# Pooling in a two-block transformer kernel: shifted sums on the vector engines replaced by a constant matrix behind the group weights

## The chip, the cores and the metric
The kernel runs on one core of a Trainium2 chip. The metric is the device time of one execution in microseconds (us); 2959.66 is the median of three runs of the kernel before.

## What is computed
Two blocks of layers work on 256 latent tokens and 256 context tokens of width 1024. The change touches the mixer of the first layer alone, which runs once, on all 512 tokens:

```python
def pool_mix(h, w, scale):                       # h: normalised, modulated
    ...
    for gi, win in enumerate(POOL_WINDOWS):      # 2, 4, 8, 16
        lo = jnp.clip(t - win // 2, 0, n - 1)
        hi = jnp.clip(t - win // 2 + win - 1, 0, n - 1)
        sl = slice(gi * POOL_GW, (gi + 1) * POOL_GW)
        csg = cs[:, :, sl]
        mean = (csg[:, hi + 1] - csg[:, lo]) / (hi - lo + 1)
        outs.append(mean - hf[:, :, sl])
    diff = jnp.stack(outs, axis=2)
    y = jnp.einsum('bngc,gce->bnge', diff, w).reshape(b, n, d)
    return y * scale
```

Each of four groups of 256 features takes the mean over a window of neighbouring tokens, less the token itself, and is then multiplied by its own 256x256 weights. The result, gated, is added to x. A feed-forward layer (ffn 0) runs ahead of it and another (ffn 1) behind it, each after an RMS norm.

## The kernel before, in words
Activations lie feature-major: a tile has 128 features on the partitions and 512 tokens (256 latent, 256 context) along the row; `x` has eight of them. Every large product is made of three f32r matmuls (`mm3`, lines 1995 to 1997): an operand is split into a high part (`hh`, `whi`, written by ScalarE) and the rest (`hl`, `wlo`, written by VectorE), and low x high, high x low and high x high add up in PSUM. Sums of squares (L2010), idle matmuls that only keep TensorE's clock up (`keep_clock`, L2002) and attention use plain fp32 matmuls, each of which shows as two records in the trace.

Each engine has its program written by hand in order, and semaphores join them. Weights come through three slots of 1 MB (`wraw`); SyncE loads a slot when VectorE has split the chunk that was in it (L614, waiting on `w_lo`), ScalarE copies it into `whi` (L718) and VectorE subtracts (L1147).

A norm: as each tile of `x` is final, ScalarE squares it (L722), TensorE adds the squares over the features (`sum_squares`, L2010); ScalarE takes the root (L739), VectorE the reciprocal (L1173). VectorE then scales 16 half tiles (L1181), ScalarE adds the shift (L757). In the mode "split", ScalarE's result goes into `hh`, and VectorE, three half tiles behind its own scaling, writes `hl` (L1193) and signals `h_ready`; TensorE can start with the first half tiles. In the mode "plain", used ahead of the pooling only, the result goes back into `tsq`, no `hl` is written, and VectorE waits for all 16.

The pooling before: `pool_group` (L505 to L518) copies a group of 128x1024 into a padded buffer, adds it to a shifted copy of itself once, twice, three or four times (windows 2, 4, 8, 16), multiplies by a table of reciprocals and subtracts the input. VectorE does groups 0, 1 and 3, GpSimd group 2. ScalarE rounds each result into `hh` (L1032), VectorE writes the rest into `hl` (L1571, signal `y_ready`), and TensorE makes two tiles of 128x512 for each group from 12 matmuls. VectorE adds each tile to `x` (L1216). TensorE runs 14, 4, 0 and 0 idle matmuls ahead of the four groups, besides the 7 of the norm.

GpSimd's queue also loads the weights of the modulation (`ADA`, 512 KB each) for later feed-forward layers. Since pooling uses the same memory (`scr`), it sends the eight loads for ffn 1 only when the last group has been rounded.

## Time and profile before

| | us |
|---|---|
| median of three runs (2958.22 to 2962.6) | 2959.66 |
| the profiled execution, its own time | 2946.88 |
| its span, first to last instruction | 2945.1 |
| TensorE busy | 2796.8 (95%) |
| VectorE busy | 2062.8 (70%) |
| ScalarE busy | 1022.2 (35%) |
| GpSimd busy | 98.2 (3%) |

The times of rows count from the start of the span. A busy share of the whole span is a mean over many stages; the pooling takes about 2% of it and has to be read by itself. PE is TensorE's matmuls, PEld its weight loads, which run beside matmuls; DVE is VectorE, ACT is ScalarE, POOL is GpSimd. PEclk is the granted clock as a share of 2.4 GHz.

### The profile page before, as it was taken

The page shows a single profiled execution, that of the slowest core. Times are in us where ns is not written, and L with a number is a line of the kernel's source. Part 1 is how long each engine was busy: PE and PEld are TensorE (multiplying, and loading weights), DVE is VectorE, ACT ScalarE, POOL GpSimd, SP SyncE. Part 2 cuts the span into 40 slices and gives each one's busy share as a digit, 9 for nine tenths or more (in the row PEclk, how much of TensorE's full clock was granted, in tenths as well). Part 3 has the DMA queues.
Part 4 walks back from the last instruction along what each step waited for, and adds up shares of the span by engine and source line. Part 5 has one row for each costly group of instructions (what it writes and reads, how often), then busy time and mean ns, then how long its engine had stood idle before and what let it go on. Part 6 is the DMA issues. An engine that isn't in the chain of part 4 may idle for free.

```text
span 2945.1 us, 48427 instructions
## 1 busy us (share of the span) xinstructions
PE 2796.8 (95%) x19022; PEld 2436.4 (83%) x19022; DVE 2062.8 (70%) x3047; ACT 1022.2 (35%) x1148; POOL 98.2 (3%) x160
## 2 busy tenths in 40 slices
PE   6999997999999999999999899998899989998998
PEld 4888864788878888778799899887699979986898
DVE  6877778876677777776667766656656666666566
ACT  5222232222233222233344444452144434443443
POOL 1000002000000000000000000000000000000000
PEclk9999998999999999999999999999999989998999
DMA  8444422444334344322244345421044554443354
GB/s 322 157 158 173 167 79 92 144 151 158 139 114 157 143 154 174 121 100 72 83 182 174 129 172 200 162 85 45 2 156 178 191 131 171 177 165 65 115 189 167
DMA packets 68652, 420.84 MB, mean 143 GB/s; under 512 B 7624, under 2 KB 8776, under 8 KB 26672
## 3 DMA queue, kind: packets, MB, share of 16 engines
q1 hardware_dynamic: 47984, 341.26, 31.5%
q0 software_dynamic: 20576, 78.26, 8.3%
q8 instruction: 69, 1.13, 0.2%
q14 instruction: 23, 0.19, 0.0%
HBM read 418.42 MB, written 1.07 MB: 142 GB/s over the span
## 4 chain that ended last, share of the span: by engine, by line
PE 86%; DVE 8%; ACT 3%; issue 2%; DMA 1%; SPq 0%; ACTq 0%; DVEq 0%
PE ps_o L1995 11%; PE ps_o L1997 11%; PE ps_o L1996 11%; PE ps_u L1995 8%; PE ps_u L1997 7%; PE ps_g L1995 7%; PE ps_u L1996 7%; PE ps_g L1997 7%; PE ps_g L1996 7%; PE ps_g L2010 2%; DVE wlo L1147 1%; PE ps_o L2194 1%; ACT whi L718 1%; DVE rstd L1173 1%; DVE tsq L1181 1%
## 5 line engine op out<-in xcount | busy, mean ns | idle before, releaser
L718 ACT ACTIVATE whi<-wraw 128x2048 fp32r<-128x2048 f32 x323 | 616.3, 1912 | 881.1 <-PE ps_u L1997 406.8
L1147 DVE TENSOR_TENSOR wlo<-wraw,whi 128x2048 fp32r<-128x2048 f32 x323 | 731.5, 2288 | 174.8 <-ACT whi L718 174.5
L1995 PE MATMUL ps_o<-ah,wlo 128*128 128x256 f32 (+1 forms) x1408 | 462.0, 328 | 17.1 <-issue 15.4
L1995 PE MATMUL ps_g<-hh,wlo 128*128 128x256 f32 (+1 forms) x1416 | 456.4, 322 | 20.0 <-DVE hl L1191 13.8
L1995 PE MATMUL ps_u<-hh,wlo 128*128 128x256 f32 (+1 forms) x1416 | 454.6, 321 | 2.2 <-DVE wlo L1147 2.2
L1997 PE MATMUL ps_g<-hh,whi 128*128 128x256 f32 (+1 forms) x1416 | 455.0, 321 | 0.0
L1996 PE MATMUL ps_g<-hl,whi 128*128 128x256 f32 (+1 forms) x1416 | 454.5, 321 | 0.0
L1997 PE MATMUL ps_u<-hh,whi 128*128 128x256 f32 (+1 forms) x1416 | 454.4, 321 | 0.0
L1996 PE MATMUL ps_u<-hl,whi 128*128 128x256 f32 (+1 forms) x1416 | 453.9, 321 | 0.0
L1997 PE MATMUL ps_o<-ah,whi 128*128 128x256 f32 (+1 forms) x1408 | 452.7, 322 | 0.0
L1996 PE MATMUL ps_o<-al,whi 128*128 128x256 f32 (+1 forms) x1408 | 452.1, 321 | 0.0
L1216 DVE SCALAR_TENSOR_TENSOR x<-ps_o,gcol,x 128x256 f32<-128x256 f32 x640 | 283.4, 480 | 146.0 <-PE ps_o L1997 144.3
L1995 PEld LDWEIGHTS ps_g<-hh,wlo 128*128 128x128 f32 x1416 | 267.4, 189 | 48.0 <-issue 27.6
L1995 PEld LDWEIGHTS ps_o<-ah,wlo 128*128 128x128 f32 x1408 | 265.8, 189 | 43.0 <-issue 20.4
L1995 PEld LDWEIGHTS ps_u<-hh,wlo 128*128 128x128 f32 x1416 | 267.2, 189 | 23.3 <-DVE wlo L1147 2.7
L1996 PEld LDWEIGHTS ps_o<-al,whi 128*128 128x128 f32 x1408 | 265.9, 189 | 23.8 <-issue 2.9
L1997 PEld LDWEIGHTS ps_g<-hh,whi 128*128 128x128 f32 x1416 | 267.5, 189 | 20.7
L1996 PEld LDWEIGHTS ps_g<-hl,whi 128*128 128x128 f32 x1416 | 267.5, 189 | 20.3
L1997 PEld LDWEIGHTS ps_u<-hh,whi 128*128 128x128 f32 x1416 | 266.9, 189 | 20.7
L1996 PEld LDWEIGHTS ps_u<-hl,whi 128*128 128x128 f32 x1416 | 267.1, 189 | 20.5
L1997 PEld LDWEIGHTS ps_o<-ah,whi 128*128 128x128 f32 x1408 | 265.6, 189 | 21.0
L806 ACT ACTIVATE ah<-tsq 128x512 fp32r<-128x512 f32 (+1 forms) x88 | 69.8, 793 | 469.8 <-PE ps_o L1997 459.7
(433 smaller groups left out, 3713.3 us busy)
## 6 DMA issues: line engine op xcount, KB each, us to landing
wraw<-in_W SPq DMA_DIRECT2D x324, 1024.0 KB, 4.8
scr<-in_ADA POOLq DMA_DIRECT2D x126, 512.0 KB, 3.9
scr<-bias_rows POOLq DMA_DIRECT2D x8, 384.0 KB, 8.7
x<-in_XT POOLq DMA_DIRECT2D x1, 2048.0 KB, 10.8
x<-in_MEMT POOLq DMA_DIRECT2D x2, 1024.0 KB, 6.2
cst<-in_CST POOLq DMA_DIRECT2D x1, 1511.5 KB, 7.3
cst<-in_CB POOLq DMA_DIRECT2D x1, 1024.0 KB, 5.1
out<-x SPq DMA_DIRECT2D x1, 1024.0 KB, 4.8
```

The source lines that it names most:

```text
L718: nc.scalar.activation(whi[:, n % SLOTS, :], wraw[:, n % SLOTS, :], ACT.Copy).then_inc(w_hi, 1)
L806: nc.scalar.activation(ah[:, :, 0:N], tmp[:, :, 0:N], ACT.Copy).then_inc(a_hi, 1)
L1147: tt_(wlo[:, n % SLOTS, :], wraw[:, n % SLOTS, :], whi[:, n % SLOTS, :].bitcast(f32), sub).then_inc(w_lo, 1)
L1173: nc.vector.reciprocal(rstd[:, 0:N], rstd[:, 0:N]).then_inc(nm_rstd, 1)
L1181: stt(dst, src(d)[:, HALVES[j]], A(d, j), rstd[:, HALVES[j]], mult, mult).then_inc(nm_t, 1)
L1216: ins = stt(x[:, d, HALVES[j]], src[:, HALVES[j]], gate(d, j), x[:, d, HALVES[j]], mult, add)
L1995: mm(out, a[1], b[0], start=first, stop=False)
L1996: mm(out, a[0], b[1], start=False, stop=False)
L1997: return mm(out, a[0], b[0], start=False, stop=last)
L2010: ins = mm(ps_g[:, 0, 0:N], ones, tsq[:, d * NTOK:d * NTOK + N], start=d == 0, stop=d == KT - 1)
L2194: ins = mm(att_out(g)[unit["rows"]], unit["v"][b], probs_t[a][g % 2][:, b, :], start=b == 0, stop=b == nb - 1)
```

## The change
The two linear steps change places: the group weights come first, on rows of tokens, and the pooling is then one product with a constant 256x256 matrix (`pool_m`: mean of the neighbours minus identity), loaded from memory (1 MB). The norm ahead runs in the mode "split". For a group g and a half s (256 tokens), u = 2g + s:

- `pool_project(u)`: 12 f32r matmuls with `hh`, `hl` as the stationary operand and the weights, 256 columns, as the moving one, into one of three PSUM banks; tokens are then on the partitions.
- `pool_copy(u)` on ScalarE: that bank, 128x512, to memory (`pool_z`, four buffers) as fp32.
- `pool_mean(u)`: 4 fp32 matmuls, two for each of two tiles: the first block of 128 tokens against 256 columns, the second against the 128 + reach columns in which its rows aren't zero.

```diff
@@ layout
-        quad = "p (a s u) -> p a s u"
-        pads = {...}
-        icnt = cut(scr, 3 * 1088, 4 * NX, "p (g u) -> p g u", u=NX)
+        pool_m = cut(scr, 0, 8 * NX, "p (g b n) -> p g b n", g=4, b=2)
+        pool_z = [cut(hid, 512 * i, 512, "p (b e) -> p b e", b=2) for i in range(4)]
...
+        def pool_bank(u):
+            return (ps_u[:, 0, :], ps_u[:, 1, :], ps_g[:, 1, :])[u % 3].rearrange("p (b e) -> p b e", b=2)
@@ gpsimd
             ada_loads(0)
-            pool.dma_start(icnt.rearrange("p g u -> p (g u)"), ICNT).then_inc(ic_in, 16)
...
-            pool_group(nc.gpsimd, link, pads["gpsimd"], 2).then_inc(pl_gp, 1)
-            pool.wait_ge(y_hi, 4)
+            pool.dma_start(pool_m.rearrange("p g b n -> p (g b n)"), PM).then_inc(pm_in, 16)
             ada_loads(1)
@@ scalar
-            norm(lambda d: x[:, d, :], NTOK, mod(0, 1), "plain", after(FIRST["pool", 0]), FIRST["pool", 0], part=1)
-            for g in range(4):
...
+            def pool_copy(u):
+                act.wait_ge(pl_mm, u + 1)
+                if u >= 4:
+                    act.wait_ge(mm_done, DONE[FIRST["pool", 0] - 1] + 2 * ((u - 4) // 2) + 2)
+                nc.scalar.activation(pool_z[u % 4], pool_bank(u), ACT.Copy).then_inc(pl_copied, 1)
+            def pool_between(q):
+                if q >= 9 and q % 2:
+                    pool_copy((q - 9) // 2)
+            norm(lambda d: x[:, d, :], NTOK, mod(0, 1), "split", after(FIRST["pool", 0]), FIRST["pool", 0], part=1, then=pool_between)
+            for u in range(4, 8):
+                pool_copy(u)
@@ vector
-            norm(xs_, NTOK, A_mod(0, 1), None, "plain", part=1)
-            link(pool_edges(nc.vector, pads["vector"]))
...
-            pool_group(nc.vector, link, pads["vector"], 3).then_inc(pl_diff, 1)
-            rest_pooled(2)
-            rest_pooled(3)
+            norm(xs_, NTOK, A_mod(0, 1), B_mod(0, 1), "split", part=1)
             chunks_out("pool", 0, add_to_x(NTOK, gate(0, 1), 8), late=1)
@@ tensor
-            for g in range(4):
-                keep_clock((14, 4, 0, 0)[g], BANK[3])
-                y_split()
...
+            def pool_project(u):
+                g, s = divmod(u, 2)
+                if u >= 3:
+                    pe.wait_ge(pl_copied, u - 2)
+                for b in range(2):
+                    t = slice(s * NX + b * 128, s * NX + (b + 1) * 128)
+                    for k in (2 * g, 2 * g + 1):
+                        if b == 0:
+                            pe.wait_ge(h_ready, pool_h0 + 2 * k + s + 1)
+                        ins = mm3(pool_bank(u)[:, b, :], (hh[:, k, t], hl[:, k, t]), (w[0][:, k, :], w[1][:, k, :]), k % 2 == 0, k % 2 == 1)
+                ins.then_inc(pl_mm, 1)
+            def pool_mean(u):
+                g, s = divmod(u, 2)
+                reach = POOL_WINDOWS[g] // 2
+                pe.wait_ge(pl_copied, u + 1)
+                for j in range(2):
+                    out = tile(n, 2 * g + j)
+                    for b, t in enumerate((slice(0, NX), slice(128 - reach, NX))):
+                        ins = mm(out[:, s * NX + t.start:s * NX + t.stop], pool_z[u % 4][:, b, j * 128:(j + 1) * 128], pool_m[:, g, b, t], start=b == 0, stop=b == 1)
+                    if s:
+                        ins.then_inc(mm_done, 1)
+            for u in range(3):
+                pool_project(u)
+            pe.wait_ge(pm_in, 16)
+            for u in range(8):
+                pool_mean(u)
+                if u < 5:
+                    pool_project(u + 3)
+                if u % 2:
+                    sum_squares(NTOK, u - LAG)
             norm(NTOK)
```

How the change moves instructions is shown at three places. In such rows a line is the engine's own order, with the program's line, the operation, output and inputs, the output's size, and the semaphores that it waits for. Line numbers of the changed kernel differ.

TensorE before, from the norm's 7 idle matmuls to the first group's product:

```order
L2002 MATMUL ps_u<-cst 128x512 x7
L2002 MATMUL ps_u<-cst 128x512 [waits w_lo]
L2002 MATMUL ps_u<-cst 128x512 x13
L1995 MATMUL ps_o<-hh,wlo 128x512 [waits o_free,y_ready]
L1996 MATMUL ps_o<-hl,whi 128x512
L1997 MATMUL ps_o<-hh,whi 128x512
```

and in the changed kernel, from the same 7 idle matmuls (L1963) to the first product (L1956 to L1958 are the three of `mm3`):

```order
L1963 MATMUL ps_u<-cst 128x512 x7
L1956 MATMUL ps_u<-whi,hl 128x256 [waits h_ready,w_lo]
L1957 MATMUL ps_u<-wlo,hh 128x256
L1958 MATMUL ps_u<-whi,hh 128x256
L1956 MATMUL ps_u<-whi,hl 128x256 [waits h_ready]
```

The 14 idle matmuls are gone (as are the 4 ahead of the second group), and the first product waits for half tiles of the norm instead of a pooled group. Further on, at the first mean (L2410), which stands behind three projections:

```order
L2410 MATMUL ps_o<-scr,hid 128x256 [waits o_free,pl_copied,pm_in]
L2410 MATMUL ps_o<-scr,hid 128x129
L2410 MATMUL ps_o<-scr,hid 128x256 [waits o_free]
L2410 MATMUL ps_o<-scr,hid 128x129
L1956 MATMUL ps_u<-whi,hl 128x256 [waits h_ready,pl_copied]
```

Means and projections take turns from there. Two sums of squares (L1971) stand behind the mean of u = 5, the other six behind the last mean, where four stood behind the last product before.

ScalarE before, from the norm's root to the next norm's squares:

```order
L739 ACTIVATE rstd<-ps_g,cst 128x512 [waits nm_sum]
L757 ACTIVATE tsq<-tsq,mods 128x256 [waits nm_t,ad_col]
L757 ACTIVATE tsq<-tsq,mods 128x256 [waits nm_t] x15
L718 ACTIVATE whi<-wraw 128x2048 [waits mm_done,w_here2]
L1032 ACTIVATE hh<-tsq 128x1024 [waits pl_diff] x2
L1032 ACTIVATE hh<-tsq 128x1024 [waits pl_gp]
```

and in the changed kernel, from the third pair behind the tenth half tile on (L727 is the shift, L1003 `pool_copy`, L688 the split of a weight chunk):

```order
L727 ACTIVATE hh<-tsq,mods 128x256 [waits nm_t] x2
L1003 ACTIVATE hid<-ps_g 128x512 [waits pl_mm]
L727 ACTIVATE hh<-tsq,mods 128x256 [waits nm_t] x2
L1003 ACTIVATE hid<-ps_u 128x512 [waits pl_mm]
L688 ACTIVATE whi<-wraw 128x2048 [waits mm_done,w_here2]
L1003 ACTIVATE hid<-ps_u 128x512 [waits mm_done,pl_mm]
L1003 ACTIVATE hid<-ps_g 128x512 [waits mm_done,pl_mm]
L1003 ACTIVATE hid<-ps_u 128x512 [waits mm_done,pl_mm] x2
```

Four copies (the first two stand just ahead of these rows, in the same manner) now come between half tiles of the norm; the other four come behind the split of a weight chunk and ahead of the next norm's squares.

GpSimd before, behind the loads for ffn 0:

```order
L654 DMA scr<-in_ICNT 128x1024 [waits ad_done]
L502 MEMSET hid 128x4x8 [waits o_free]
L503 MEMSET hid 128x4x8
L508 COPY hid<-tsq 128x4x256 [waits nm_hi,ic_in,pool_seq]
L509 ISA
L509 TENSOR_TENSOR scr<-hid 128x4x271 [waits pool_seq]
L514 TENSOR_TENSOR scr<-scr 128x4x269 [waits pool_seq]
L514 TENSOR_TENSOR scr<-scr 128x4x265 [waits pool_seq]
L517 TENSOR_TENSOR scr<-scr 128x4x256 [waits pool_seq]
L518 TENSOR_TENSOR tsq<-scr,tsq 128x1024 [waits pool_seq]
L633 DMA scr<-in_ADA 128x1024 [waits y_hi]
L633 DMA scr<-in_ADA 128x1024 x7
```

and in the changed kernel:

```order
L639 DMA scr<-in_PM 128x2048 [waits ad_done]
L618 DMA scr<-in_ADA 128x1024 x8
L618 DMA scr<-in_ADA 128x1024 [waits ad_done] x3
L632 UNCONDITIONAL_BRANCH
L632 ISA
```

The load of the matrix takes the place of that of the reciprocals, and eight loads no longer wait for the pooling: they follow at once.

## Rows read from the trace of the kernel before
**Rows 1.** The page: the chain of work that ended last, by engine
```profile
PE 86%; DVE 8%; ACT 3%; issue 2%; DMA 1%; SPq 0%; ACTq 0%; DVEq 0%
```
**Rows 2.** Stretches: length; busy PE, PEld, DVE, ACT, POOL; PEclk, DMA share, GB/s
```profile
447.00:460.00 13.00, 0.00 (x0) 0.00 (x0) 12.83 (x7) 1.06 (x1) 8.60 (x3) 0.58 0.17 71
460.00:472.00 12.00, 8.21 (x19) 5.50 (x20) 11.76 (x11) 2.00 (x2) 0.00 (x0) 0.60 0.00 0
472.00:487.00 15.00, 13.56 (x49) 8.88 (x48) 9.95 (x20) 5.57 (x9) 4.25 (x8) 1.00 0.72 274
```
**Rows 3.** Timeline, VectorE in the pooling (start, duration, line, what)
```profile
409.84 4.49 DVE L1147 TENSOR_TENSOR wlo<-wraw,whi 128x2048 fp32r<-128x2048 f32 x2
...
433.39 6.42 DVE L1181 SCALAR_TENSOR_TENSOR tsq<-x,acol,rstd 128x256 f32<-128x256 f32 x16
...
445.05 2.27 DVE L508 COPY scr<-tsq 128x1024 f32<-128x1024 f32 x1
```
**Rows 4.** Timeline, TensorE in the pooling and at the next norm
```profile
428.33 18.19 PE L2002 MATMUL ps_u<-cst 128*128 128x512 f32 x42
463.79 0.80 PE L1995 MATMUL ps_o<-hh,wlo 128*128 128x512 f32 x1 [17.27 <-DVE hl L1571]
...
486.21 3.59 PE L2010 MATMUL ps_g<-tsq,cst 128*128 128x512 f32 x8
...
496.96 0.47 PE L1995 MATMUL ps_g<-hh,wlo 128*128 128x512 f32 x1 [1.15 <-DVE hl L1193]
```
**Rows 5.** Timeline, VectorE and ScalarE at the next norm, in mode split
```profile
489.84 0.69 ACT L739 ACTIVATE rstd<-ps_g,cst 128x512 f32<-128x512 f32 x1 [1.89 <-PE ps_g L2010]
...
493.95 1.67 DVE L1181 SCALAR_TENSOR_TENSOR tsq<-x,acol,rstd 128x256 f32<-128x256 f32 x4
...
495.54 0.48 DVE L1193 SCALAR_TENSOR_TENSOR hl<-tsq,mods,hh 128x256 fp32r<-128x256 f32 x1
...
505.05 1.67 DVE L1193 SCALAR_TENSOR_TENSOR hl<-tsq,mods,hh 128x256 fp32r<-128x256 f32 x4
```
**Rows 6.** Timeline, TensorE on token rows in the attention's projections
```profile
1292.32 0.28 PE L1995 MATMUL ps_o<-hh,wlo 128*128 128x256 f32 x1
...
1294.71 0.28 PE L1997 MATMUL ps_o<-hh,whi 128*128 128x256 f32 x1
```
**Rows 7.** Timeline, TensorE's fp32 matmuls of 128 and 256 columns in attention
```profile
1411.74 1.06 PE L2194 MATMUL ps_o<-hid,scr 128*128 128x128 f32 x8
1412.63 0.60 PE L2180 MATMUL ps_o<-cst,tsq 128*128 128x128 f32 x4
...
1417.12 1.92 PE L2380 MATMUL ps_o<-hid,cst 128*40 128x256 f32 x8
1418.88 1.03 PE L2380 MATMUL ps_o<-big,cst 128*40 128x256 f32 x4
```
**Rows 8.** Groups by line: ScalarE's copy of a PSUM bank to memory
```profile
L857 ACT ACTIVATE hid<-ps_o 128x512 f32<-128x512 f32 x16 | 9.6, 598 | 17.6 <-PE ps_o L2180 17.6
```
**Rows 9.** Timeline, TensorE in a later norm's tail, at the lower and the higher clock
```profile
1658.07 0.41 PE L1996 MATMUL ps_o<-al,whi 128*128 128x256 f32 x1
...
1658.92 0.41 PE L1997 MATMUL ps_o<-ah,whi 128*128 128x256 f32 x1
...
1661.10 0.60 PE L2010 MATMUL ps_g<-tsq,cst 128*128 128x256 f32 x2
...
1662.24 0.60 PE L2010 MATMUL ps_g<-tsq,cst 128*128 128x256 f32 x2
```
**Rows 10.** Weight loads of the L2194 matmuls: count, duration min/median/max
```profile
L2194 PEld LDWEIGHTS ps_o<-hid,scr x128: 186/192/338, 1298.0 to 1429.1; 128*128 128x128 f32 x128
```
**Rows 11.** GpSimd's queue: the wait ahead of the pooling, the loads behind it
```profile
426.04 0.12 POOL L502 MEMSET hid<- 128x32 f32 x1 [30.61 <-DVE x L1216]
474.67 4.25 POOL L633 DMA_DIRECT2D scr<-in_ADA  x8 [18.91 <-ACT hh L1032]
```
**Rows 12.** A stretch of the last attention, columns as in rows 2
```profile
2674.70:2698.60 23.90, 20.34 (x61) 14.57 (x60) 11.15 (x22) 5.05 (x13) 2.25 (x3) 0.50 0.32 33
```

More of the change, by code:

```diff
@@ L722, in square, with norm @@
                 nc.scalar.activation(tsq[:, d * NTOK:d * NTOK + N], src(d)[:, 0:N], ACT.Square).then_inc(nm_sq, 1)
-            def norm(src, N, B, mode, ready, n, part=None, squared=False, again=False, memory=None, early=False):
+            def norm(src, N, B, mode, ready, n, part=None, squared=False, again=False, memory=None, early=False, then=None):
                 k = st["k"]
@@ L752, in norm @@
                         src_t = tsq[:, d * NTOK + j * NX:d * NTOK + (j + 1) * NX]
-                        dst = src_t if mode == "plain" else hh[:, d, HALVES[j]]
+                        dst = hh[:, d, HALVES[j]]
                         if B is None:
@@ L757, in norm @@
                             nc.scalar.activation(dst, src_t, ACT.Identity, bias=B(d, j)).then_inc(nm_hi, 1)
-                        st["h"] += mode == "split"
+                        st["h"] += 1
+                        if then is not None:
+                            then(2 * d + j)
                     if memory is not None and d % 4 == 3:
@@ L2424, in _ @@
             ffn(0, NTOK)
[L2425 removed]
+            norm(NTOK)
             n = FIRST["pool", 0]
             w = weights(chunk(n), 256)
[L2428 to L2436 removed]
+            pool_h0 = st["h"] - 2 * KT
+            def pool_project(u):
[13 more added lines that the diff above has]
+                pe.wait_ge(pl_copied, u + 1)
+                for j in range(2):
+                    out = tile(n, 2 * g + j)
[12 more added lines that the diff above has]
+                    sum_squares(NTOK, u - LAG)
             norm(NTOK)
```

72 lines of the change are left out of this document (12 added, 60 removed).

## The prediction
> **What bounds the kernel now.** I read the chain of waits first: 86% of it is TensorE [rows 1], so a saving counts only where TensorE waits. The table by stretch shows one such place in the pooling: TensorE does nothing from 447 to 460 us while VectorE is busy 12.83 of 13 us, and its granted clock falls to the lower of its two levels (1.2 of 2.4 GHz; 0.58 is the mean of the stretch, 0.60 of the next [rows 2]). The timelines give the reason. Scaling for the norm starts at 433.39, the first pooled group at 445.05 [rows 3], TensorE's idle matmuls run out near 446.5, and the first product waits 17.27 us for the `hl` of a pooled group, until 463.79 [rows 4]. The last product ends near 486.2, four sums of squares follow, and ScalarE takes the next norm's root at 489.84 [rows 4, 5]. From 433.39 to 489.84 is 56.45 us; this is the stretch that the change rewrites. What lies ahead of 433.39 and behind 489.84 keeps its instructions, and I move the latter as a block.
>
> **When operands come.** The norm now runs in mode split, as the next norm does. There, scaling starts at 493.95, the first `hl` starts at 495.54, the thirteenth at 505.05, and one takes 0.48 [rows 5]: half tile q (0 to 12) is there 2.07 + 0.79q us after the start. Started at 433.39, half tile 2, which projection 0 needs, is there at 437.0, half tile 6 (projection 2) at 440.2, and the sixteenth 12.8 us after the start, at 446.2.
>
> **What TensorE does instead.** A projection is 12 f32r matmuls of 256 columns with token rows as the stationary operand. The attention runs the same form: 20 steps from 1292.32 to 1294.71, 0.12 us each [rows 6], so a projection is 1.43 us. A mean is two tiles of one 256-column and one 129- to 136-column fp32 matmul. An fp32 matmul leaves two records (the 21 idle matmuls give 42 [rows 4]). Eight records of 128 columns go by in 1412.63 - 1411.74 = 0.89 us, 0.11 each; eight of 256 columns in 1418.88 - 1417.12 = 1.76 us, 0.22 each [rows 7]. A mean is then 2 x (2 x 0.22 + 2 x 0.11) = 1.32 us. The widths of 129 to 136 columns aren't in the trace: bounds are 0.11 and, as if they cost like 256 columns, 0.22, which would add 8 x 4 x 0.11 = 3.5 us; I take 0.11, whose width is nearest.
>
> The sum by the clock: projections 0 and 1 are done near 439.7; projection 2 gets its last operand at 440.2 and ends with its last nine matmuls near 441.4. From then on operands and copies are ahead of TensorE, and it runs 8 means (10.6), 5 projections (7.1) and two sums of squares (2 x 0.86, a record being 0.43 by 18.19 us for 42 [rows 4]: 1.7), with about 0.5 us for the first of these sums, whose square on ScalarE stands behind copy 7. The last mean ends at 441.4 + 19.9 = 461.3. Six sums are left (5.1), against four before: 466.4, and the root starts near 466.6 instead of 489.84. That is **-23.2 us**.
>
> Two small terms against it. Changing between f32r and fp32 sixteen times: one fp32 sum and six f32r matmuls of 256 columns repeat every 1.14 us [rows 9], and 0.43 + 6 x 0.12 is 1.15, so by this row it is free; I allow 0.3 in all. The clock: the 18 idle matmuls that went with the pooling are gone, so behind the norm's 7 (14 records, ended by about 434.4) TensorE idles some 1.1 us, does three matmuls, and idles 1.1 again until 437.0. Before the next norm's first product it idled 1.15 us and the granted clock stayed high; before the pooling it fell in the 17.27 us of idling [rows 4]. The gap here is nearer to the first. If the clock falls all the same, it comes back after some 6 us of work: the mean of 0.60 between 460 and 472 us [rows 2] is 9.6 us at 0.5 and 2.4 at 1, so it rose near 469.6, after products that began at 463.79. Six us at half speed cost 3. I allow 1 us. Forecast: **-22 us**, with bounds of -23.2 and -16.5 (wide records and one fall of the clock).
>
> **What is hidden.** ScalarE's eight copies take 0.60 each [rows 8]. Copies 0 to 3 stand between steps of the norm on ScalarE and push its end back, but only once TensorE has two projections in hand. The split of a weight chunk behind copy 3 (on VectorE 4.49 us for two, 2.25 for one [rows 3]) lies beside means 0 to 2; VectorE's additions to x wait behind it, and a mean needs a freed bank only from the fifth tile on, some 9 us later. VectorE loses all of its shifted sums and GpSimd its group; both would stand idle, at no gain of their own. The weights of the pooling are split by 414.3 [rows 3].
>
> GpSimd's queue moves: its wait ahead of the pooling began at 426.04 - 30.61 = 395.4, so the matrix (1 MB) and the eight loads of 512 KB that were issued at 474.67 [rows 11] now start there. At the 274 GB/s of the stretch in which those loads ran before [rows 2], 5.2 MB take 19 us, until about 415, far ahead of the first mean at 441.4. Weight chunks issued meanwhile, after the split at 409.84 [rows 3], are wanted behind the next norm: no cost.
>
> **Rivals.** (1) The hand-offs are not hidden: each mean waits for its copy. A copy of 0.60 with 0.3 us of signals, eight times, is 7.2 us: -15 us, 2944.7. For it: mean u needs copy u, and there are only three banks. Against it: the order puts two projections between a projection and its mean.
>
> (2) The fp32 weight loads lie open. Sixty-four records of fp32 each load 128 columns anew, 0.19 us a load [rows 10]; if none ran under the matmul ahead, that is 64 x 0.19 = 12.2 us: -10 us, 2949.7. Against it: the L2194 matmuls, of the same shape, step 0.11 us with loads of 0.19 [rows 7, 10], so the loads overlap. The Trainium skill ("TensorE: Matmul & The Clock Gate", section "Weight-path perf modes — Fast Weight Load (FWL) and DoubleRow") says that the fast weight load is for types other than FP32, which speaks against putting fp32 tiles on the weight side. By that rule this rival would hold; the trace has 0.19 us for the load and a step shorter than it.
>
> (3) Slower: the clock falls in the gaps ahead of 437 us and stays at 1.2 GHz until the next feed-forward layer starts. For it: with short matmuls TensorE was busy 20.34 of 23.9 us in the last attention and the clock stayed at 0.50 [rows 12]; against it: in the pooling before, it rose after 6 us of f32r work. Its price: a 256-column step is 0.21 [rows 9], so everything doubles. Projection 2 ends at 444.8; 8 means, 5 projections and 2 sums take 21.3 + 12.7 + 3.4 us, the six sums 10.3: root at 492.7, +2.9. The next norm's seven idle matmuls then take 12 us instead of 6 and end near 504.5, when the first operand is there at 496.96 + 2.9 = 499.8: +4.7 more, +7.6 in all, 2967.3. It decides only if the clock is still low at the root: a fall of 6 us costs 3.
>
> (4) The stretch is hidden: something else releases the next layer, and nothing changes, 2959.7. Against it, every step from 433.39 to 489.84 has its releaser in the rows of the pooling itself.
>
> **How the numbers follow.** The profiled execution took 2946.88 us (span 2945.1), so the changed one should show about 2925 (span 2923). The median of the runs shown is 12.8 us above it; I take the same saving off the median: 2959.66 - 22 = **2937.7**. Chances: forecast 0.82, rival 1 0.07, rival 2 0.05, rival 3 0.04, rival 4 0.02. The forecast's own range is 2959.66 - 23.2 and - 16.5, with 3 us at the low and 1 us at the high end for the runs' scatter (4.4 us between the three) and for falls of the clock elsewhere, which may come out otherwise when all that follows is moved: 2933 to 2944. With rival 1's 2944.7 the range is 2933 to 2945. A change of over 0.2% (5.9 us) can be told from none in a measurement of this kernel: faster by more than that are the forecast and rivals 1 and 2, 0.94; within it rival 4, 0.02; slower rival 3, 0.04.
>
> **What would show it.** In the changed kernel's timeline: projection 0 done by about 438.3 us, means from about 441.4, f32r steps of 0.12 and fp32 steps of 0.22 and 0.11, the last mean near 461 and the root near 466.6; granted clock 1.00 from 437 on; the pooling's copies never the releaser of a mean from u = 1 on. Means whose start is released by ScalarE speak for rival 1, fp32 steps of 0.3 to 0.4 us for rival 2, a clock of 0.5 over the stretch for rival 3, and a root at 466 with an unchanged start of the next layer's products for rival 4. The forecast is wrong if the root comes later than 474 us, or if the time behind the root grows.

## The result, and the profile after

The changed kernel took 2931.56 us (median of five runs, 2922.3 to 2938.2), against 2959.66: the ratio is 0.9905, with a 95% interval of 0.9892 to 0.9918, or 28.1 us less. The forecast was 2937.7 with a range of 2933 to 2945, so the time lies 1.4 us below the range. The profiled execution took the same 2931.56 (span 2929.9), only 15.3 us less than the profiled execution of before. The experiments had to bring these two differences, 28 and 15, together.

The pooling itself came out as predicted. The chain of waits names VectorE less than it did [rows 1]:

```profile
PE 89%; DVE 7%; ACT 2%; issue 2%; DMA 1%; SPq 0%; ACTq 0%; DVEq 0%
```

The two stretches in which TensorE had stood still or crawled [rows 2] are now full, and the granted clock (the column behind POOL) is 1.00:

```profile
447.00:460.00 13.00, 13.00 (x85) 11.39 (x84) 7.27 (x14) 6.71 (x12) 0.00 (x0) 1.00 0.23 82
460.00:472.00 12.00, 12.00 (x38) 6.36 (x37) 5.41 (x6) 2.16 (x4) 0.00 (x0) 1.00 0.00 0
```

TensorE's timeline from the first projection to the next layer's first product answers to [rows 4]. L2410 is the mean, L1971 the sums of squares, L1963 idle matmuls; between means stand projections, which are left out here:

```profile
436.64 0.36 PE L1956 MATMUL ps_u<-whi,hl 128*128 128x256 f32 x1 [1.10 <-DVE hl L1172]
...
442.47 1.47 PE L2410 MATMUL ps_o<-scr,hid 128*128 128x256 f32 x8
445.22 1.47 PE L2410 MATMUL ps_o<-scr,hid 128*128 128x256 f32 x8
447.97 1.47 PE L2410 MATMUL ps_o<-scr,hid 128*128 128x256 f32 x8
...
456.21 1.48 PE L2410 MATMUL ps_o<-scr,hid 128*128 128x256 f32 x8
457.67 1.98 PE L1971 MATMUL ps_g<-tsq,cst 128*128 128x512 f32 x4
459.49 2.82 PE L2410 MATMUL ps_o<-scr,hid 128*128 128x256 f32 x16
462.14 5.31 PE L1971 MATMUL ps_g<-tsq,cst 128*128 128x512 f32 x12
...
474.60 0.47 PE L1956 MATMUL ps_g<-hh,wlo 128*128 128x512 f32 x1 [1.14 <-DVE hl L1172]
```

A bracket gives the time for which the engine was idle before the row, and what ended it; no mean has one. From one mean's start to the next are 2.75 us, the sum of the mean (1.32) and the projection (1.43) that the prediction worked out. ScalarE's timeline shows the reverse of rival 1, a copy (L1003) that waits for TensorE, and the root (L709):

```profile
450.91 0.60 ACT L1003 ACTIVATE hid<-ps_g 128x512 f32<-128x512 f32 x1 [1.99 <-PE ps_g L1958]
...
467.49 0.69 ACT L709 ACTIVATE rstd<-ps_g,cst 128x512 f32<-128x512 f32 x1 [3.49 <-PE ps_g L1971]
```

The norm's scaling began at 434.43 in this execution (433.39 before [rows 3]). Counted from there, the numbers of the forecast stand beside those measured:

| from the start of the scaling, us | forecast | measured |
|---|---|---|
| first mean | 8.0 | 8.04 |
| last mean done (the sums behind it start) | 27.9 | 27.7 |
| root (56.45 before) | 33.2 | 33.06 |
| from the root to the next layer's first product (7.12 before) | 7.1 | 7.11 |

To see where the rest of the time came from, I cut each execution at ScalarE's norm roots. "Pooling" below is the stretch from the root ahead of the pooling to the one behind it; "dilated" is the stretch between the two roots around the last attention; "rest" is the span without these two.

| profiled execution | pooling | dilated | rest | span |
|---|---|---|---|---|
| before | 61.31 | 125.42 | 2758.4 | 2945.1 |
| after | 37.92 | 132.51 | 2759.5 | 2929.9 |

The pooling gave 23.4 us, and the dilated stretch took 7.1 back. That stretch has the same instructions in both kernels. **Theory A**: the gain is in the pooling alone, and what differs elsewhere is the granted clock, which falls in some executions and not in others. **Theory B**: the change gives some 5 us more behind the pooling.

### The profile page after: what moved, and what is told of

Its sections match the earlier page's. It is cut to its first block, busy times and chain, and to the rows that moved or that the text cites. A ratio compares the mean times of both kernels' runs of the same rounds, so it can differ in the third digit from the quotient of the medians.

```text
span 2929.9 us, 48578 instructions
## 1 busy us (share of the span) xinstructions
PE 2797.9 (95%) x19098; PEld 2444.8 (83%) x19098; DVE 2037.9 (70%) x3041; ACT 1022.4 (35%) x1152; POOL 81.4 (3%) x152
## 4 chain that ended last, share of the span: by engine, by line
PE 89%; DVE 7%; ACT 2%; issue 2%; DMA 1%; SPq 0%; ACTq 0%; DVEq 0%
PE ps_o L1956 11%; PE ps_o L1958 11%; PE ps_o L1957 11%; PE ps_u L1956 8%; PE ps_u L1958 8%; PE ps_u L1957 8%; PE ps_g L1956 8%; PE ps_g L1958 7%; PE ps_g L1957 7%; PE ps_g L1971 2%; DVE wlo L1126 1%; PE ps_o L2155 1%; DVE rstd L1152 1%; DVE tsq L1160 1%; ACT whi L688 1%
## 5 line engine op out<-in xcount | busy, mean ns | idle before, releaser
L688 ACT ACTIVATE whi<-wraw 128x2048 fp32r<-128x2048 f32 x323 | 616.5, 1912 | 879.9 <-PE ps_u L1958 406.3
L1956 PE MATMUL ps_o<-ah,wlo 128*128 128x256 f32 (+1 forms) x1408 | 464.1, 330 | 17.1 <-issue 15.5
L1956 PE MATMUL ps_g<-hh,wlo 128*128 128x256 f32 (+1 forms) x1416 | 455.9, 322 | 19.6 <-DVE hl L1170 13.8
L1956 PE MATMUL ps_u<-hh,wlo 128*128 128x256 f32 (+1 forms) x1416 | 454.4, 321 | 2.2 <-DVE wlo L1126 2.2
L1958 PE MATMUL ps_g<-hh,whi 128*128 128x256 f32 (+1 forms) x1416 | 454.3, 321 | 0.0
L1958 PE MATMUL ps_u<-hh,whi 128*128 128x256 f32 (+1 forms) x1416 | 453.9, 321 | 0.0
L1958 PE MATMUL ps_o<-ah,whi 128*128 128x256 f32 (+1 forms) x1408 | 453.9, 322 | 0.0
L1956 PEld LDWEIGHTS ps_g<-hh,wlo 128*128 128x128 f32 x1416 | 266.8, 188 | 48.4 <-issue 28.0
L1956 PEld LDWEIGHTS ps_o<-ah,wlo 128*128 128x128 f32 x1408 | 267.1, 190 | 43.4 <-issue 20.5
L1956 PEld LDWEIGHTS ps_u<-hh,wlo 128*128 128x128 f32 x1416 | 267.0, 189 | 23.4 <-DVE wlo L1126 2.6
L1958 PEld LDWEIGHTS ps_o<-ah,whi 128*128 128x128 f32 x1408 | 267.1, 190 | 21.0
L1958 PEld LDWEIGHTS ps_g<-hh,whi 128*128 128x128 f32 x1416 | 267.0, 189 | 20.6
L1958 PEld LDWEIGHTS ps_u<-hh,whi 128*128 128x128 f32 x1416 | 266.7, 188 | 20.6
```

The lines of the kernel that those rows point to most:

```text
L688: nc.scalar.activation(whi[:, n % SLOTS, :], wraw[:, n % SLOTS, :], ACT.Copy).then_inc(w_hi, 1)
L1956: mm(out, a[1], b[0], start=first, stop=False)
L1958: return mm(out, a[0], b[0], start=False, stop=last)
```

## The experiments

**The same kernels again.** Nothing was changed in `b_again`, nor in `a_again`.

> The kernel before, nothing changed: a second profiled execution of it. Theory A (the change saves its 23.4 us in the pooling alone; the rest of the measured 28, and the scatter, is the granted clock, which falls to 0.50 for a length that varies from execution to execution, above all in the stretch between the norm roots around the dilated attention, 125.4 us in the profiled execution of before and 132.5 us in that of the change): the stretch from the norm root ahead of the pooling to the one behind it takes 61.3 +- 1 us again; if the whole is near 2959 instead of 2946.9, then some 10 us more lie in stretches with the clock at 0.50, most of them around the dilated attention (125.4 grows to 132 or more). Theory B (the change gives some 5 us more behind the pooling): the stretches behind the pooling add up to 2435 us again within 2 us, and no stretch between two norm roots differs by over 2 us from the first profiled execution.

> The changed kernel, nothing changed: Theory A: the pooling's stretch (norm root to norm root) takes 37.9 +- 0.5 us again, timed runs scatter between 2920 and 2940 as before, and the profiled execution's difference to the first one (2931.6) lies, to within 2 us, in stretches with other lengths of the clock at 0.50. Theory B: the median is 2931.6 +- 2 and the ratio to the kernel before 0.9905 +- 0.0005 once more, whatever the clock shows.

| profiled execution | pooling | dilated | rest | span |
|---|---|---|---|---|
| b_again | 62.90 | 125.43 | 2769.0 | 2957.3 |
| a_again | 37.92 | 125.46 | 2761.3 | 2924.7 |

The medians were 2954.70 us (eight runs) and 2928.58 us (four runs).

The dilated stretch of the changed kernel came back to 125.46. Its rows, in the first and in this execution, have the same number of matmul records and another clock:

```profile
2598.02:2730.53 132.51, 117.00 (x673) 94.31 (x672) 71.12 (x127) 51.51 (x102) 3.20 (x4) 0.85 0.31 76
```

```profile
2598.29:2723.75 125.46, 111.10 (x673) 89.98 (x672) 71.07 (x127) 51.54 (x102) 3.21 (x4) 0.89 0.32 80
```

For before, theory A was wrong in its detail. The second execution was 12.2 us longer, but not in the dilated stretch: 10.6 us lie in the rest, in steps of 1.2 to 2.9 us in seven stretches and one step back, and 1.6 us in the pooling itself. Behind a wait of TensorE in front of the last two groups the clock fell a second time, which it hadn't in the first execution. TensorE's timeline of `b_again`, the sum of squares (L2010) and the product behind it:

```profile
476.99 2.08 PE L2010 MATMUL ps_g<-tsq,cst 128*128 128x512 f32 x2 [2.72 <-ACT tsq L722]
478.07 1.42 PE L1995 MATMUL ps_o<-hh,wlo 128*128 128x512 f32 x1
```

In the first execution the same wait was 1.44 us:

```profile
477.13 1.13 PE L2010 MATMUL ps_g<-tsq,cst 128*128 128x512 f32 x2 [1.44 <-ACT tsq L722]
```

The same stretch by windows, first the execution that the prediction was made from, then `b_again`:

```profile
472.00:480.00 8.00, 6.56 (x26) 4.26 (x24) 7.04 (x13) 3.67 (x6) 4.25 (x8) 1.00 0.49 171
```

```profile
472.00:480.00 8.00, 5.28 (x15) 3.29 (x14) 6.62 (x11) 3.67 (x6) 4.24 (x8) 0.81 0.53 190
```

So the saving in the pooling is 23.4 us against the first execution and 25.0 us against this one.

**Idle matmuls in the dilated attention**, in both kernels (`b_keep`, `a_keep`), to take its scatter away:

```diff
+                    if s == 7:
+                        keep_clock(5, BANK[0])
                     if s >= 1:
                         flip(s - 1)
...
                     if t == 3:
+                        keep_clock(5, BANK[0])
                         head_spread(4)
...
                 for u in range(8):
+                    if u >= 2:
+                        pe.wait_ge(at_y, AT0[3] + u - 2)
+                    keep_clock(4 if u else 12, ps_o[:, 2 + (u + 1) % 2, 128:384])
                     flip(u)
```

> The kernel before, with idle matmuls in the dilated attention where TensorE waits (5 ahead of each of the two later spreads of the head norms, 12 x 256 columns ahead of the first turn of the last attention, 4 x 256 columns ahead of each later one), nothing else changed. They are meant to hold the granted clock there. Theory A: the clock stays at 1.00 from the spread on, the stretch around the dilated attention falls from 125.4 to 110 to 118 us, the whole to 2930 to 2942, and the timed runs agree within 5 us. Theory B: the stretch shortens alike, and the difference to the changed kernel with the same idle matmuls is 28 us.

> The changed kernel with the same idle matmuls in the dilated attention. Theory A: the stretch around the dilated attention takes the same 110 to 118 us as in the kernel before with them, the scatter of the timed runs falls from 16 to 5 us or less, the whole is 2908 to 2918 us, and its median lies 23.4 +- 2 us under that of the kernel before with the idle matmuls. Theory B: it lies 28 +- 2 us under it. If the idle matmuls don't hold the clock (it falls as long as before), the scatter stays and this pair tells nothing.

The stretch was expected to fall to between 110 and 118 us. It became longer, 135.55 and 135.50 us, although the granted clock there rose to 0.96. The idle matmuls were too long for the waits that they filled: an idle matmul leaves two records, and 12 of 256 columns took 7.10 us where TensorE had waited 2.83 us in the changed kernel. TensorE's timeline of `a_keep`:

```profile
2671.37 7.10 PE L1963 MATMUL ps_o<-cst 128*128 128x256 f32 x24
```

and its dilated stretch by windows:

```profile
2600.10:2735.60 135.50, 130.46 (x773) 104.26 (x772) 71.51 (x127) 51.48 (x102) 3.21 (x4) 0.96 0.30 74
```

As a pair they still served: medians of 2964.92 and 2937.71, means of 2964.9 (7 runs) and 2937.4 (5 runs), a difference of 27.5 +- 2.8 us (twice the standard error), with a scatter of 8 and 5 us. Theory A had asked for 23.4 +- 2, theory B for 28 +- 2, so this speaks for B in the size; but the pooling took 62.97 and 37.93, so 25.0 of it lie there and not behind it.

**One projection, one mean.** `e_alt` takes away the lead of the projections; the sums of squares all stand behind the last mean.

```diff
-            for u in range(3):
-                pool_project(u)
             pe.wait_ge(pm_in, 16)
             for u in range(8):
+                pool_project(u)
                 pool_mean(u)
-                if u < 5:
-                    pool_project(u + 3)
-                if u % 2:
-                    sum_squares(NTOK, u - LAG)
```

> The changed kernel with projection and mean of each unit in turn (P0 M0 P1 M1 ...), so that every mean stands right behind its own projection and must wait for ScalarE's copy of it; the sums of squares all behind the last mean. Read in the stage: from the start of the norm's scaling to the root behind the pooling the change took 33.1 us (434.4 to 467.5). Theory A (TensorE has no gap there because projections run three units ahead; a hand-off to the copy and back costs 0.6 us for the copy and 0.2 to 0.4 us around it): eight hand-offs of 0.8 to 1.0 us, the stage 6 to 8 us longer, the root 39.5 to 41 us behind the start of the scaling, and the copies are named as releasers of the means. Rival (hand-offs run beside the matmul pipeline and cost next to nothing): under 2 us longer.

The root came 47.3 us after the start of the scaling, 14.2 more: twice what was expected (the whole, run once: 2938.96 us). TensorE's timeline shows the hand-offs and what came on top:

```profile
442.41 2.94 PE L2410 MATMUL ps_o<-scr,hid 128*128 128x256 f32 x8 [2.46 <-ACT hid L1003]
448.60 1.58 PE L2410 MATMUL ps_o<-scr,hid 128*128 128x256 f32 x8 [0.69 <-ACT hid L1003]
452.28 1.58 PE L2410 MATMUL ps_o<-scr,hid 128*128 128x256 f32 x8 [0.69 <-ACT hid L1003]
455.98 1.58 PE L2410 MATMUL ps_o<-scr,hid 128*128 128x256 f32 x8 [0.69 <-ACT hid L1003]
460.98 2.26 PE L2410 MATMUL ps_o<-scr,hid 128*128 128x256 f32 x8 [2.00 <-DVE x L1192]
466.29 1.58 PE L2410 MATMUL ps_o<-scr,hid 128*128 128x256 f32 x8 [0.69 <-ACT hid L1003]
```

An undisturbed unit takes 3.69 us instead of 2.75, so a hand-off shows 0.94, as expected; the seven steps between eight means make 6.6. The steps from 442.41 and from 460.98 are 6.19 and 5.31 us long, at a clock that had fallen to 0.50 (4.1 us over 3.69 together); the fifth mean waited 2.00 us for VectorE's additions to x, and the step ahead of it was 1.3 longer. Two projections more stand behind the first mean (2.9 us), which itself starts only 0.5 us sooner, 7.50 us behind the start of the scaling instead of 8.04: 2.3. Together that is 14.3, for the 14.2 measured. The two sums that moved cost nothing by moving: they take about 1.8 us of TensorE in either place. So the lead of three projections is worth more than its hand-offs: it also puts work into the wait for the first operands, and it avoids the waits of 2.46 and 2.00 us, around which the clock fell.

**All copies behind the norm** (`e_late`):

```diff
-            norm(lambda d: x[:, d, :], ..., part=1, then=pool_between)
-            for u in range(4, 8):
+            norm(lambda d: x[:, d, :], ..., part=1)
+            for u in range(8):
                 pool_copy(u)
```

> The changed kernel with ScalarE's first four copies not between the norm's tiles but all behind its last one (nothing else moved). Theory A: ScalarE's last tile of the norm is done near 448; copies from there, so the first mean starts near 448.5 to 449 instead of 442.5, TensorE idles some 6 us, and the stage ends 5 to 7 us later (the root 38 to 40 us behind the start of the scaling); if the idle time pulls the granted clock down, up to 3 us more. Rival (the copies' place doesn't matter, because the means are not what the end waits for): under 1 us.

The root came 42.0 us after the start of the scaling, 8.9 more (the whole, run once: 2935.40 us). The first mean stood at 447.03, 14.1 us behind the start instead of 8.04; the other 2.9 us are the clock, whose mean over the 11 us from 436 was 0.81 and over the next 13 us 0.77.

```profile
447.03 2.90 PE L2410 MATMUL ps_o<-scr,hid 128*128 128x256 f32 x8 [5.89 <-issue]
```

The row calls this wait "issue", yet the mean waits for `pl_copied`, as ScalarE's timeline shows:

```profile
444.56 1.89 ACT L688 ACTIVATE whi<-wraw 128x2048 fp32r<-128x2048 f32 x1
446.36 1.06 ACT L1003 ACTIVATE hid<-ps_u 128x512 f32<-128x512 f32 x2
```

The first two copies began at 446.36 and took 1.06 together. A wait under that name can be one for a semaphore. More moved here than the four copies: the split of a weight chunk (L688, 1.89 us), which stood behind copy 3, now stands ahead of them all, and 1.8 of the 6.1 us by which the first mean is later are its time.

**Wide means** (`e_wide`), 256 columns instead of 129 to 136 in the second block:

```diff
-                    for b, t in enumerate((slice(0, NX), slice(128 - reach, NX))):
+                    for b, t in enumerate((slice(0, NX), slice(0, NX))):
```

> The changed kernel with the second half of each mean at the full 256 columns instead of 129 to 136 (the added columns multiply zeros of the matrix; the result is the same). Theory A (the fp32 mean costs TensorE 0.11 us per 128 columns and record, two records per matmul, and TensorE alone bounds the stage): 16 matmuls x 2 records x about 124 columns, 0.1 us each, so 3.2 us more, less what a gap takes up; the root 36 to 36.6 us behind the start of the scaling instead of 33.1. Rival (the rate of the mean is set by its weight loads of 0.19 us, not by its columns): under 1 us more.

The root came 36.10 us after the start of the scaling, 3.04 more, against 3.2 expected (the whole, run once: 2932.81 us). One unit takes 3.16 instead of 2.75 us (448.13 to 451.29 and on to 454.45):

```profile
448.13 1.89 PE L2410 MATMUL ps_o<-scr,hid 128*128 128x256 f32 x8
451.29 1.89 PE L2410 MATMUL ps_o<-scr,hid 128*128 128x256 f32 x8
454.45 1.89 PE L2410 MATMUL ps_o<-scr,hid 128*128 128x256 f32 x8
```

The four records of the two widened matmuls cost 0.10 us more each, for about 124 columns. Here an fp32 mean is paid by its columns, not by its weight loads, of which there are as many as before.

**Sums of squares as f32r** (`e_fast`), in the norm behind the pooling only:

```diff
-                nc.scalar.activation(tsq[:, d * NTOK:d * NTOK + N], src(d)[:, 0:N], ACT.Square)...
+                nc.scalar.activation(hh[:, d, 0:N] if fast else tsq[:, d * NTOK:d * NTOK + N], src(d)[:, 0:N], ACT.Square)...
...
+            nc.scalar.activation(ah[:, 0, 0:128], ones, ACT.Copy)
...
-                    ins = mm(ps_g[:, 0, 0:N], ones, tsq[:, d * NTOK:d * NTOK + N], start=d == 0, stop=d == KT - 1)
+                    a, b = (ah[:, 0, 0:128], hh[:, d, 0:N]) if st["k"] == 2 else (ones, tsq[:, d * NTOK:d * NTOK + N])
+                    ins = mm(ps_g[:, 0, 0:N], a, b, start=d == 0, stop=d == KT - 1)
```

> The changed kernel with the sums of squares of the norm behind the pooling as f32r instead of fp32 (ScalarE's squares written as f32r into the normalised activations' buffer, which is free by then, and a copy of the matrix of ones as f32r), nothing else changed. Theory A (from the first projection to the root TensorE is the bound of the stage, so work taken off it comes off the time): eight sums of 0.885 us become 0.21 us each, of these the last six stand behind the last mean: 4 us less once the last residual and square (some 1.3 us) are exposed, the root 28.5 to 29.5 us behind the start of the scaling instead of 33.1, the whole 4 us less. Rival (residuals on VectorE and squares on ScalarE end last, the sums only fill the wait): under 1 us less.

The root came 29.40 us after the start of the scaling, 3.66 less, where 4 were expected. The last six sums have one record each instead of two, and now the last square on ScalarE ends last:

```profile
461.65 1.72 PE L1973 MATMUL ps_g<-hh,ah 128*128 128x512 f32 x5
463.65 0.51 PE L1973 MATMUL ps_g<-hh,ah 128*128 128x512 f32 x1 [0.28 <-ACT hh L692]
```

TensorE is the bound of the new stage up to there, so work taken off it came off the time until ScalarE's squares became the last to end. The whole was 2924.72 us (median of four runs, 2921.69 to 2929.55; ratio to before 0.9892, 0.9865 to 0.992).

**The clock alone, in the kernel before** (`b_clock`):

```diff
-                keep_clock((14, 4, 0, 0)[g], BANK[3])
+                keep_clock((31, 4, 0, 3)[g], BANK[3])
```

> The kernel before with more idle matmuls in the pooling: 31 instead of 14 ahead of the first group's projection and 3 instead of none ahead of the last group's, so that TensorE is not idle while VectorE builds the sums. It asks how much of the pooling's gain is the granted clock alone (before: 20.5 us of the pooling at 0.50 in every profiled execution, 24 in two of three) and how much is VectorE's work. Theory A (VectorE's chain of shifted sums sets the end; the clock adds only the second fall in front of the last group): the clock stays at 1.00, and the stretch from root to root is 60 to 61.5 us instead of 61.3 to 63.0, so the clock alone is worth 0 to 2 us of the 24.5 and the rest is VectorE's work moved off the path. Rival (the slow projections were the price): the stretch falls to 56 us or less.

The pooling took 65.54 us, longer, and the whole 2956.58 (median of ten runs), the same as before. The idle matmuls ran until about 460.7 us (76 records from 427.91, 32.78 us), and the mean clock of the stretch rose from 0.83 (in the first execution) to 0.95, but the first product started at 463.40 as before, behind VectorE:

```profile
463.40 0.79 PE L1995 MATMUL ps_o<-hh,wlo 128*128 128x512 f32 x1 [2.72 <-DVE hl L1571]
...
476.74 1.89 PE L2010 MATMUL ps_g<-tsq,cst 128*128 128x512 f32 x2 [2.60 <-ACT tsq L722]
...
483.80 2.74 PE L2002 MATMUL ps_u<-cst 128*128 128x512 f32 x6
```

I put the three late idle matmuls in the wrong place. The wait is at 476.74, ahead of the third product; they stood ahead of the last, where nothing waited, and cost about 2.6 us (six records of 0.43). Without them it is 62.9 to 63.0, as in the other executions.

The clock wasn't high throughout: it had fallen again when the first product came (0.57 on average from 463 to 467 us). So this run alone doesn't say what the products at full clock would be worth. Three executions together do. The window is the time from the start of the scaling to the sum of squares that waits for ScalarE (477.13, 476.99 and 476.74 above), in the first execution, `b_again` and `b_clock`:

```profile
433.39:477.13 43.74, 25.03 (x63) 13.38 (x61) 40.71 (x44) 13.13 (x23) 18.78 (x11) 0.77 0.09 31
433.25:476.99 43.74, 23.75 (x64) 12.54 (x62) 40.71 (x44) 13.13 (x23) 18.78 (x11) 0.80 0.10 31
432.97:476.74 43.77, 38.45 (x97) 19.06 (x95) 40.74 (x44) 13.13 (x23) 18.81 (x11) 0.96 0.10 32
```

It takes 43.7 us at a mean clock of 0.77, 0.80 and 0.96, with VectorE busy for 40.7 of them: up to there VectorE's work was the price, as the chain said, and the clock was worth nothing. Behind it TensorE sets the time, and the clock counts: from there to the root are 12.7 us in the first execution, at full clock, and 14.3 in `b_again`, with the second fall. (The expectation's 20.5 us of low clock hold for the pooling of every unchanged execution of before; for 24 a fall outside the pooling has to be counted in.)

**More executions.** `a_third` is the changed kernel again; `e_best` is `e_fast` with a few idle matmuls in the dilated attention:

```diff
+                    if s == 7:
+                        keep_clock(3, BANK[0][:, 0:256])
                     if s >= 1:
                         flip(s - 1)
...
                 scores(1)
+                keep_clock(6, ps_o[:, 3, 0:256])
                 for u in range(8):
```

> The changed kernel once more, for the mean over more executions. Theory A: the pooling's stretch takes 37.9 us a third time, and the mean of all timed runs of the changed kernel lies 24 to 27 us under the mean of all timed runs of the kernel before (2956), not 28 or more. Theory B: 28 or more.

> The changed kernel with the f32r sums of squares in the norm behind the pooling, and with few idle matmuls in the dilated attention: 3 x 256 columns ahead of the turn in front of the last spread and 6 x 256 columns ahead of the first turn of the last attention (one of 256 columns took 0.25 us at full clock in the run with too many of them, and twice the records of that length count). Theory A on the pooling: its stretch takes 34.3 us as in the run with the f32r sums alone. On the dilated attention: the earlier idle matmuls took 10.5, 7.1 and 14 us of TensorE where it had waits of 1.2, 2.8 and 0.5 us per turn, which is why they cost 10 us although the clock was low for 10 us instead of 27; with 1.3 and 2.6 us of them the stretch should be 116 to 123 us instead of 125.4, and the whole 2914 to 2922. Rival: the clock falls there for the lack of rows in the spread and the scores, not for the waits; then the stretch stays at 125 to 132 us and the whole at 2922 to 2927.

`a_third`: pooling 37.93, dilated 131.88, median 2925.58 (2922.74 to 2935.93). `e_best`: pooling 34.27, a second time as with f32r sums alone; dilated 123.95 at a clock of 0.93, under the 125.4 to 132.7 of the executions without idle matmuls there, but not in the 116 to 123 expected:

```profile
2602.82:2726.77 123.95, 111.44 (x691) 91.26 (x690) 70.98 (x127) 51.56 (x102) 3.21 (x4) 0.93 0.33 81
```

Its median is 2925.35 (four runs, 2923.79 to 2930.85), the same as `e_fast`. By the pooling's stretch the f32r sums are worth 3.66 us, twice, and the mean of the runs of `e_fast`, 2925.2, fits that beside 2929.0 for all runs of the changed kernel (below). That the idle matmuls add anything isn't shown.

**What was still open**: timed runs gave 27.5 us, the pooling 23.4 or 25.0. Three more executions of before and one of the changed kernel, unchanged:

> The kernel before, unchanged, for its stretches in one more execution. By now the mean of the timed runs puts the saving at 27.5 us (24.2 to 30.7) while the pooling's stretch gives 23.4 against the first profiled execution of before (61.3) and 25.0 against two others (62.9, 63.0). Theory A: the pooling's stretch is 62.9 in most executions of before, or longer, and everything else adds up to the same in both kernels (2890.5 us on average in before without the idle matmuls, 2891 in the changed kernel). Theory B: the pooling is 62 or less in most, and the rest of before is 3 us longer than in the changed kernel.

> The same as the run before it: theory A, pooling's stretch 62.9 or longer and the rest near 2890; theory B, 62 or less and the rest near 2894.

> The same once more: theory A, pooling's stretch 62.9 or longer and the rest near 2890; theory B, 62 or less and the rest near 2894.

> The changed kernel, unchanged, beside them: both theories have the pooling's stretch at 37.9 us; theory A has the rest near 2891, theory B near 2888 or less.

| profiled execution | pooling | dilated | rest | span |
|---|---|---|---|---|
| b_p1 | 62.94 | 132.50 | 2769.1 | 2964.5 |
| b_p2 | 62.94 | 125.43 | 2760.5 | 2948.8 |
| b_p3 | 62.90 | 132.73 | 2762.7 | 2958.3 |
| a_p1 | 37.93 | 125.43 | 2760.3 | 2923.7 |

The pooling is as theory A had it. The dilated stretch of before, too, is 125.4 in some and 132.6 in other executions. The second fall of the clock in the pooling of before is the rule: four of the five unchanged executions have it, and the one that the prediction was made from has not. Against those four the pooling's gain is 25.0 us.

All timed runs together: 98 of before with a mean of 2957.5 (2946.2 to 2966.2), 16 of the changed kernel with a mean of 2929.0 (2922.3 to 2938.2), 28.5 us less with a 95% interval of 25.6 to 31.4; the expectation of `a_third` had 24 to 27 for theory A and 28 or more for B. Outside the pooling, the mean over the five executions of before and `b_clock` is 2892.2 +- 2.7 (standard error), and over eight of the changed kernel and its variants (`e_alt`, `e_wide`, `e_late` and `e_fast`) 2889.3 +- 1.4: 3.0 +- 3.0 less, which is what theory B asked of the last three executions of before, within an error as large as itself. Theory B's 5 us are not ruled out by this, and no stretch carries them. The one right behind the pooling took 380.4 to 380.9 us in every execution of before, and 379.2 in two and 380.5 in two of the changed kernel's four; on average 0.9 us less. The granted clock goes with it: in the two of 379.2 it doesn't fall in this stretch, in the two of 380.5 it falls once (0.91 from 820 to 840 us), and in every execution of before it falls once (0.89 from 530 to 545 us in `b_again`, 0.91 from 845 to 865 us in the first). Whether the change keeps that fall away or chance did, and what the other 2 us are, stays open.

## Why the prediction was right about the stage and missed its range

**What bounds the kernel**: right. VectorE's work sets the first 43.7 us of the pooling behind the start of the scaling, at any of three mean clocks. What no run shows is how much of it VectorE lost to GpSimd's group beside it (below).

**The sum of TensorE's work**: right, term by term. Operands arrived as predicted (first mean 8.04 us after the start of the scaling, 8.0 forecast), a unit took 2.75 us, the means were paid by columns at the value chosen (0.11 for a record of 129 to 136 columns; `e_wide` showed 0.10 more for the width that was the bound), the six sums took 5.3 us for 5.1. The root came after 33.06 us for 33.2. (Of the bounds, -16.5 should be -16.7 by its own terms, 23.2 less 3.5 and 3; the range is the same.)

**The two allowances** of 0.3 us for changing between f32r and fp32 and 1 us for the clock weren't needed. TensorE waited 1.10 and 0.90 us ahead of the first projections and the clock stayed at 1.00. So the saving was 23.4 and not 22 against the profiled execution.

**What was called hidden** was hidden: copies wait for TensorE; additions to x and the split of a weight chunk delay no mean. Both covers are real, though: with the lead of the projections gone, the hand-offs (0.94 each) and a wait of 2.00 us for VectorE's additions appear at once in `e_alt`, and with the copies late the stage is 8.9 us longer in `e_late`. The loads that moved on GpSimd's queue were issued from 394.70 on; the DMA share from 400 to 410 us was 0.95 where it had been 0.00, and TensorE had a single wait of 2.5 us between 385 and 432 us, the same as before. From the norm's root ahead of ffn 0 to the one ahead of the pooling, `e_late`, with the loads moved, took 377.15 us and `b_again` 377.11. Holding them back wasn't tried.

**Rivals.** (1) fell; its price of 7.2 us for exposed hand-offs was right for the hand-offs (6.6 in `e_alt`) and too low for losing the lead, 14.2 in all. (2) fell: the Trainium skill ("TensorE: Matmul & The Clock Gate", section "Weight-path perf modes — Fast Weight Load (FWL) and DoubleRow") gives the fast weight load to types other than FP32. That sentence says nothing on whether a load runs beside the matmul ahead of it, so the prediction's "By that rule this rival would hold" took more from it than it states. The eight fp32 loads of a mean took 0.19 us each and lay beside matmuls: the unit of 2.75 us has no room for 1.5 us more, and `e_wide` makes columns the price. (3) and (4) fell: the clock was 1.00, and the next layer began 7.11 us behind the root as before.

**The step that failed** is the one from the stage to the whole, "I take the same saving off the median", with "3 us at the low" end for scatter. Two of its terms were too small.

The first is the saving itself, 23.2 at most. It was worked out from the one execution of before at hand, in which the clock doesn't fall ahead of the last two groups; in the four others it does, and against them the pooling gave 25.0. The prediction noted that this execution was 12.8 us under the median, but treated the difference as something outside the stretch that the change rewrites. Of it, 1.6 us were inside: the second fall of the clock, which goes with the change.

The second is the allowance for scatter. With 25.0 in the place of 23.2 the low end would still have been 2931.7, just above the 2931.56 measured. Three runs of before, 4.4 us apart, gave no view of it: the timed runs of before have a mean of 2957.5, 2.2 below the median that the forecast started from, and the changed kernel's first five runs spread over 16 us, with a standard deviation of 5.3, or 2.4 for a mean of five. The two granted clocks of the dilated attention, 7 us apart, were one source of it.

So of the 6.1 us between 2937.7 and 2931.56, 1.4 are the allowances and the rounding of the stage, 1.6 the second fall, and the remaining 3.1 have no place in a stretch: they lie within the scatter of the medians. The miss wasn't bad luck of one set of runs, though. The other medians of the changed kernel (2928.58, 2925.58 and 2925.19) lie lower still, and the 3.0 +- 3.0 us outside the pooling are the part of the 28.5 whose cause stays open.

## What to carry to other kernels

When the profiled execution is faster than the timed runs, ask which stretch makes the difference before taking a saving off the median: a fall of the clock behind a wait that the change removes belongs to the saving. When two kernels differ in one place, cut the executions at fixed points and compare the pieces; four executions of the changed pooling agreed within 0.02 us while the timed runs scattered over 16. And an idle matmul that is to hold the clock must be shorter than the wait it fills: with 12 of them in a wait of 2.83 us the clock rose and the time grew.

## What the runs showed that was not expected

The dilated stretch takes about 125.4 or about 132 us in unchanged executions of both kernels, with the same 673 matmul records, at a mean clock of 0.89 or of 0.83 to 0.85 (127.9 in `e_wide` and `e_fast`). In the pooling of before, a better clock early on was followed by a worse one later: in `b_again` it was 0.72 instead of 0.60 between 460 and 472 us, so TensorE was through with its second group sooner and waited 2.72 us instead of 1.44, and behind the longer wait the clock was at 0.50. All six executions of before and its variants with 2.6 to 2.8 us there had this fall. A wait of such a length isn't enough by itself: the one of 2.53 us near 410 us, in the layer ahead, was followed by a fall in some executions (mean clock 0.79 from 408 to 416 us in the first of the changed kernel) and not in others (1.00 in the first of before and in `a_again`).

A low clock over idle time cost nothing: in `b_clock` the mean clock of the pooling rose from 0.83 to 0.95 and no product came sooner for it.

VectorE's first group went slowly beside GpSimd's. The same instructions in VectorE's first group and in its second, in the first execution of before, with GpSimd's last one:

```profile
447.36 2.93 DVE L509 TENSOR_TENSOR scr<-scr 128x1084 f32<-128x1084 f32 x1
450.32 3.25 DVE L517 TENSOR_TENSOR scr<-scr 128x1024 f32<-128x1024 f32 x1
452.56 3.20 POOL L518 TENSOR_TENSOR tsq<-scr,tsq 128x1024 f32<-128x1024 f32 x1
...
457.48 1.29 DVE L509 TENSOR_TENSOR scr<-scr 128x1084 f32<-128x1084 f32 x1
460.12 1.22 DVE L517 TENSOR_TENSOR scr<-scr 128x1024 f32<-128x1024 f32 x1
```

With the copy (2.27 and 0.68) and the subtraction (3.25 and 1.23), four instructions took 11.7 us while GpSimd was at work and 4.4 behind it. By VectorE's own times GpSimd's group would have cost it about 7.0 us, an estimate from these rows and the 1.28 of L514; beside it, VectorE lost about 7.3. So the help of GpSimd was worth next to nothing here, if the two did slow each other. No run takes GpSimd's group away, so that isn't shown, and neither is how much of the saving of 25.0 a kernel before without it would have left.
